# Where the projection's dense blocks stand inside the six solver levels of a gated delta rule

## What the kernel computes

```python
m = jnp.where(strict, beta[..., :, None] * kk * decay, 0.0) + jnp.eye(C, dtype=f32)
rhs = jnp.concatenate([v * beta[..., None], k * (beta * jnp.exp(gc))[..., None]], axis=-1)
sol = lax.linalg.triangular_solve(m, rhs, left_side=True, lower=True, unit_diagonal=True)
u0, w = sol[..., :dv], sol[..., dv:]
...
def step(state, inp):
    u = u0_c - jnp.einsum("bhcd,bhde->bhce", w_c, state)
    o = jnp.einsum("bhcd,bhde->bhce", qd_c, state) + jnp.einsum("bhcj,bhje->bhce", qk_c, u)
```

## Time and profile before

| | value |
|---|---|
| median of 3 runs | 3722.05 us (3721.0 to 3726.62) |
| the profiled execution's own time | 3725.82 us |
| its span in the trace | 3724.0 us |
| TensorE busy | 3395.2 us, 91% of the span |
| VectorE, ScalarE, GpSimd busy | 41%, 23%, 48% |
| mean granted TensorE clock | 0.969 of full speed |

### The profile page before, as it was taken

One profiled execution on the slowest core, in us unless ns is written; L12 is line 12 of the kernel. 1 busy time (PEld: TensorE's weight loads), 2 busy tenths in 40 slices (PEclk: granted clock), 3 DMA queues, 4 the chain that ended last, 5 costly groups with the idle time before them and its releaser, 6 DMA issues.

```text
span 3724.0 us, 47370 instructions
## 1 busy us (share of the span) xinstructions
PE 3395.2 (91%) x17232; PEld 2797.9 (75%) x17232; DVE 1524.5 (41%) x2077; ACT 841.8 (23%) x1269; POOL 1786.0 (48%) x1828
## 2 busy tenths in 40 slices
PE   7699989999999999999979998999988888879897
PEld 6667777887788778877768786777767777658685
DVE  2442234444444443444342213344345555541523
ACT  4322123223322332233220101111122222210111
POOL 4545544234433443334315675666654544436574
PEclk9899999999999999999989999999999999999998
DMA  5212221111111111111124223222221112232122
GB/s 207 102 63 85 91 74 57 51 60 70 68 39 64 65 68 51 56 62 68 59 94 152 86 101 124 97 84 91 96 96 59 64 68 70 90 113 101 68 99 81
DMA packets 53364, 306.69 MB, mean 82 GB/s; under 512 B 5012, under 2 KB 7188, under 8 KB 21812
## 3 DMA queue, kind: packets, MB, share of 16 engines
q1 hardware_dynamic: 33984, 247.48, 19.1%
q10 hardware_dynamic: 19316, 58.32, 4.2%
HBM read 284.74 MB, written 21.04 MB: 82 GB/s over the span
## 4 chain that ended last, share of the span: by engine, by line
PE 73%; DVE 14%; ACT 6%; issue 5%; POOL 1%; DMA 1%; ACTq 0%; DVEq 0%; POOLq 0%; SPq 0%
PE gemm_ps L388 18%; PE gemm_ps L390 18%; PE gemm_ps L389 18%; DVE arena L774 9%; ACT arena L1417 3%; DVE arena L780 3%; PE bankC L517 3%; PE bankA L505 3%; PE bankB L515 2%; PE bankA L674 1%; POOL w_lo L346 1%; ACT L1417 1%; DVE a_lo L774 1%; PE bankB L562 1%; PE bankB L563 1%
## 5 line engine op out<-in xcount | busy, mean ns | idle before, releaser
L388 PE MATMUL gemm_ps<-a_hi,w_hi 128*128 128x512 f32 (+1 forms) x3744 | 1516.8, 405 | 116.0 <-DVE a_lo L774 83.3
L390 PE MATMUL gemm_ps<-a_hi,w_lo 128*128 128x512 f32 (+1 forms) x3744 | 1451.8, 388 | 0.0
L389 PE MATMUL gemm_ps<-a_lo,w_hi 128*128 128x512 f32 (+1 forms) x3744 | 1449.8, 387 | 0.0
L361 POOL CAST w_hi<-w_raw 128x512 fp32r<-128x512 f32 x880 | 544.6, 661 | 1825.3 <-issue 1819.3
L346 POOL TENSOR_TENSOR w_lo<-w_raw,w_hi 128x512 fp32r<-128x512 f32 x944 | 1249.5, 1354 | 70.1 <-ACT w_hi L1417 70.1
L388 PEld LDWEIGHTS gemm_ps<-a_hi,w_hi 128*128 128x128 f32 x3744 | 718.1, 192 | 283.0 <-DVE a_lo L774 72.3
L390 PEld LDWEIGHTS gemm_ps<-a_hi,w_lo 128*128 128x128 f32 x3744 | 716.3, 191 | 143.8
L389 PEld LDWEIGHTS gemm_ps<-a_lo,w_hi 128*128 128x128 f32 x3744 | 719.1, 192 | 127.8 <-issue 9.6
L774 DVE TENSOR_TENSOR arena<-gemm_ps,arena 128x512 f32<-128x512 f32 (+3 forms) x145 | 96.0, 662 | 803.2 <-PE gemm_ps L390 798.7
L774 DVE RECIPROCAL arena<-arena 128x512 f32<-128x512 f32 (+2 forms) x70 | 172.7, 2468 | 361.8 <-ACT arena L1417 359.9
L1417 ACT ACTIVATE arena<-arena 128x512 f32<-128x512 f32 (+5 forms) x334 | 204.4, 612 | 437.2 <-DVE arena L774 423.3
(11 more groups left out here) (151 smaller groups left out, 2225.5 us busy)
## 6 DMA issues: line engine op xcount, KB each, us to landing
w_raw<-w_stream SPq DMA_DIRECT2D x236, 1024.0 KB, 4.8
y_scratch<-arena ACTq DMA_DIRECT2D x20, 512.0 KB, 3.5
arena<-y_scratch ACTq DMA_DIRECT2D x15, 512.0 KB, 3.6
arena<-gc_scratch ACTq DMA_DIRECT2D x12, 512.0 KB, 3.6
arena<-x_t ACTq DMA_DIRECT2D x1, 4096.0 KB, 13.3
arena<-y_scratch ACTq DMA_DIRECT2D x1, 4096.0 KB, 25.5
x_scratch<-arena ACTq DMA_DIRECT2D x1, 4096.0 KB, 13.2
y_out<-arena ACTq DMA_DIRECT2D x4, 1024.0 KB, 3.9
```

Of the source, the lines that this page charges most:

```text
L361: pool.tensor_copy(part(w_hi, w, q), part(w_raw, w, q)).then_inc(pool_step, 1)
L388: pe.matmul(o, hi, a_hi[:, k, 0:width], start=(k == 0), stop=False)
L389: pe.matmul(o, hi, a_lo[:, k, 0:width], start=False, stop=False)
L390: last = pe.matmul(o, lo, a_hi[:, k, 0:width], start=False, stop=(k == KT - 1))
```

## The change

The table of steps gets other weights in the levels. Before, each of the four steps of a level has 0.75; after, the half step of value head 0 has 2, that of value head 1 has 0, the whole step of value head 0 has 1, that of value head 1 has 0.

```diff
 DN_STEPS = ([("natural", 10), ("values", 8), ("transposed", 6)]
-            + [(s, l, a, 0.75) for l in range(1, LEVELS) for s in ("half", "whole") for a in range(2)]
+            + [(s, l, a, w) for l in range(1, LEVELS)
+               for s, a, w in (("half", 0, 2), ("half", 1, 0), ("whole", 0, 1), ("whole", 1, 0))]
             + [("solved", 6)]
```

## The result

The changed kernel takes 3681.06 us in the median of 4 runs (3679.77 to 3684.19), against 3722.79 us for the kernel before (3721.0 to 3726.62; the three runs quoted ahead and a fourth, 3723.53). The ratio is 0.9886 with a 95% interval of 0.9871 to 0.9901: 41.7 us, 1.1%, faster. The forecast was 3688 us with a range of 3680 to 3706. The profiled execution took 3684.19 us, its span is 3682.4 us.

What follows compares the result with a forecast made beforehand. TensorE, the chain that ended last, was taken as the bound. 22.1 us from the levels plus 12.0 from the clock made 34.1 us, from a median of 3722.05 to 3688 us, range 3680 to 3706.

Steps and rivals of the forecast that it cites:

- Part 1, the second half step's wait: In the levels, value head 1's half step no longer waits for VectorE's copies: 0.53 us less a level.
- The 0.27 us to spare: VectorE's copies free the second half step 3.79 us after the second whole step's start; it is due at 4.06.
- Part 2, tile 1's eviction in ScalarE's way: At level 3 ScalarE's copy queues behind the eviction: new 1.36 us TensorE wait, level 0.12 us longer.
- Sum of parts 1 and 2: Levels 2 to 6: 1.77 us gained a trip, 19.5 in eleven; with the twelfth list's 2.65, together 22.1 us.
- The part that the twelfth list was to give: In the twelfth list ScalarE evicts nothing, so levels 2 to 6 gain 0.53 us each: 2.65 us.
- Part 3, the clock: Behind line 562's wait, 7 of eleven 3.41 us half-clock stretches go, 1.71 us each: 12.0 us.
- Line 685's rate: Later in the kernel, five of eight 2.79 us waits precede a clock drop; by that rate 4 of eleven would go.
- The falls that stay: Rival: every loop trip keeps its half-clock stretch behind line 562; only 22.1 us gained, 3700 us; chance 0.28.
- A half step that still waits: Rival: value head 1's half step still waits in the levels; some 11 us gained, 3711 us; chance 0.09.
- The new wait bringing a fall of its own: One way to the no-gain rival: a half-clock stretch behind level 3's new wait, 18.8 us lost, 3719 us; chance 0.06.
- VectorE's copies ahead of the taps: Rival: at level 3 value head 0's copies precede the taps, second whole step waits about 5.4 us; 3744 us; chance 0.03.

Runs made afterwards that it cites:

- the run with its old order: Changed kernel with four more dense blocks ahead of head_out and level 3 alone in its old step order: 3655.99 us.
- two kernels without falls: Kernel before and changed kernel, each with four more dense blocks ahead of head_out, taking out the 2.64 us wait: 3674.82 and 3656.78 us.
- the kernel with 1.79 us of filler: Changed kernel with the second group of solved's small matmuls done twice in the eleven loop trips: 3720.48 us.
- the late Silu: Changed kernel with ScalarE doing tile 1's Silu behind the copy to T1 of value head 1 at level 3: 3683.47 us.
- the kernel before with more work: Kernel before with both groups of solved's small matmuls done twice in the eleven loop trips: 3758.69 us.
- the late Silu kernel with filler: Changed kernel with tile 1's Silu behind the next copy to T1, and seven of solved's small matmuls done twice: 3693.87 us.

## Why the prediction was right

**Part 1, the second half step's wait.** Right: 0.53 us computed for levels 2, 5 and 6, and level 2 takes the 7.43 us that were put together from old rows. The 0.27 us to spare held in every trip: no half step waits for VectorE's copies any more.

**Part 2, tile 1's eviction in ScalarE's way.** Right: a new wait in each of eleven trips and none in the twelfth list, the whole step 4.72 us after tile 1 is complete. It was due at 3.37, so the wait is 1.35 us by start times; the profile counts it as 1.18, since it models the ends of matmuls, and that is under the 1.3 to 1.5 that the profile was to show. Level 3 is neither gain nor loss, as the run with its old order shows.

**Sum of parts 1 and 2.** 1.77 us a trip computed, 1.76 measured between two kernels without falls; in all 22.1 us computed, against 20.2 between the spans of these two and 18.0 between their medians. The part that the twelfth list was to give, 2.65 us, isn't clear: it took 150.60 us before and 146.45 after, 2.4 us less once the old fall's 1.71 is taken off, but the two kernels without falls differ by only 0.65 us there.

**Part 3, the clock.** The mechanism was right, and it was the term that was mis-sized: 7 falls gone, 12.0 us, where the profile has all 11 gone, 18.8 us. With 18.8 in its place the sum is 40.9 us; 41.7 were measured. The reasoning for 7 was weak in both directions. Line 685's rate described another loop with other lengths. What carried was that trips of one length repeat whatever their wait met. That 119.43 us is such a length was luck as far as the prediction goes: it had no row for it, and a trip of 118.0 us without a fall would have kept all eleven. That the falls hang on the length and not on the waits that the change removed is shown by the kernel with 1.79 us of filler (eleven falls back) and by the late Silu (eleven back, with one wait less).

**Where the wait must lie for a fall.** The traces show this better than the lengths of the trips do. The falls keep a spacing of their own. In the late Silu kernel the starts of the eleven falls are 119.46 or 119.47 us apart, each time, while the ends of the waits are 119.44 to 119.52 apart; in the kernel before it is 122.88 against 122.71 to 122.91, and in the kernel before with more work it is 126.29 or 126.30 against 126.01 to 126.07, but for the one place without a fall. Over the seven traces that have falls there are 77 of the 2.64 us waits and 61 falls, and all 61 begin between 0.62 us before the wait's end and 1.44 us after it. For the 16 waits without a fall, a neighbouring fall of the same trace can be carried on by one or two of these three distances to the start that would lie nearest to the wait's end. It is 0.89 to 1.57 us before the wait's end in seven, and 1.46 to 1.59 us after it in nine. The two groups don't overlap.

The lengths follow. The changed kernel's trips of 119.43 us are 0.04 short of 119.47, so each wait lies where the one before it did, and none of them falls. An estimate from the same numbers: a trip with a fall would take 121.1 us, 1.7 more than 119.47, and the places that fall are 2.1 us wide in all, so one or two falls would have carried the wait out of them, wherever the loop began. With a fall in it the old trip is 122.86, next to 122.88. And a length can steer itself: a fall that begins inside the wait costs less, so the late Silu's trips of 118.0 us settle where the fall costs the 1.5 us that make 119.5. Filler that makes them 126.03 walks 0.26 us a trip against 126.29, which are the falls at 0.55 to 1.33.

**The rivals.** The falls that stay, 3700: not so. A half step that still waits: not so. The new wait bringing a fall of its own: not so, the clock is 1.00 in whole trips. VectorE's copies ahead of the taps: its list was unchanged.

**What stays open.** The changed kernel's trace has no fall in the loop from which the position of its waits could be measured, so that they lie clear is inferred from the other kernels. Why a wait is followed by a fall at some positions and not at others isn't shown. Whether a kernel's count of falls is the same in every execution was seen only in the profiled ones and in the mean clocks; in the late Silu kernel with filler it is not.

## What to carry to other kernels

Put a loop's schedule together from start-to-start distances of old rows, one term for each pair of neighbours; here that gave new levels to 0.01 us, and a moved eviction's cost too, once the other engines' lists had been compared as well. Look at the clock column before and after every change to a loop whose TensorE waits about as long once a trip as it did here (2.64 us): a gain or a loss of 1.7 us a trip can come from the trip's length alone, and it can hide or double what an edit is worth. To measure edits in such a loop, first take out the wait; here the late Silu was then worth 1.45 us a trip, against 1.46 computed for its wait, and the change itself 1.76, against 1.77.

## What the runs showed of the hardware

The same 2.64 us wait of TensorE is followed by 3.4 us at 1.2 GHz in all trips of one kernel and in none of another, and in some trips of a third. The low stretch begins up to 1.4 us after the wait's end, when TensorE is busy again (a wait that ends at 858.47 in the kernel before with more work has its low stretch from about 859.5). The falls of a kernel follow each other at 119.47, 122.88 or 126.29 us, more evenly than its waits do, and whether a wait is followed by one goes with where it lies against that spacing (61 waits with a fall and 16 without, whose places don't overlap). The Trainium skill (TensorE: Matmul & The Clock Gate, What's actually happening) calls the activity window free-running; the traces agree, in that neither the wait's length nor its place in the program decides. Two kernels that are about 1.45 us of waiting a trip apart (the changed kernel and the late Silu) therefore took the same time, and 19.7 us of added matmuls cost 39 us in one kernel and 14 in the other.
